# Softmax weights divided before they are turned, values as the stationary operand, and head outputs split in place for the output projection

## The chip, the cores and the metric

The program runs on one core of one Trainium2 chip (trn2). It is one launch. The metric is the device time of that launch in microseconds (us), the median of a few executions. Beside it there is one profiled execution, whose trace is read here.

The engines have short names: PE is TensorE (products; PEld its weight loads), DVE is VectorE, ACT is ScalarE, POOL is GpSimd, SP is SyncE, which issues the DMAs.

## The reference

Two blocks of two layers each run one after the other on 256 tokens of width 1024 in float32. The first block (gated linear attention, a dense and a mixture-of-experts feed-forward) is not touched by the change. Of the second block these parts matter:

```python
def causal_block_attention(score_fn, v):
    def one_block(blk):
        start = blk * BLOCK_Q                      # 128 queries
        s = score_fn(start)
        q_pos = start + jnp.arange(BLOCK_Q)
        s = jnp.where(k_pos[None, :] <= q_pos[:, None], s, -jnp.inf)
        w = jax.nn.softmax(s, axis=-1).astype(v.dtype)
        return jnp.einsum('bhqk,bkhd->bqhd', w, v)

# layer 0, "fox": 16 heads of 64 columns
cum = jnp.cumsum(jax.nn.log_sigmoid(f_logit), axis=1).transpose(0, 2, 1)
s = q_t . k_s * FOX_HEAD_DIM ** -0.5 + cum[t] - cum[s]
mix = o.reshape(B, S, D_MODEL) @ w_o               # 1024 x 1024

# layer 1, "mla": 16 heads, 128 + 64 score columns, 128 value columns
s = (q_nope . k_nope + q_rope . k_rope) * (QK_NOPE_DIM + QK_ROPE_DIM) ** -0.5
mix = o.reshape(B, S, MLA_HEADS * V_HEAD_DIM) @ w_o   # 2048 x 1024
```

Each of the two attentions is followed by its output product with `w_o`, a residual and a layer norm, and then a feed-forward layer whose weights (2816 wide) are streamed from memory.

## The kernel before

**Order of the work.** `stages()` lists the steps of the program. Each engine runs through the same list in its own block of code, in order, and the engines meet at semaphores only. No scheduler moves anything. `Tally` counts how often each semaphore will have been raised when a step begins (`n.g`, `n.act` and so on). The steps around the change are, for layer 0, `fox`, `trs8 "src"`, `out1`, `ln`, and for layer 1, `mla`, `trs16 "src"`, `out2`, `ln`.

**Products of linear layers.** Float32 operands are split into a high half (rounded to fp32r, a TensorE input format) and a low half (the rest). A product is then three fp32r products: high by high, high by low, low by high. Activations stand as `u_hi`/`u_lo` (1024 wide) or `y_hi`/`y_lo` (2048 wide). ACT writes the high half, DVE subtracts it for the low half. Weights come by DMA into `wide` and are split piece by piece, 128 x 1024 each, into the two-deep ring `l_hi`/`l_lo` (the last chunk also into `out_hi`/`out_lo`). Plain float32 products are used in the attentions. In the trace one plain float32 product stands as two MATMUL records, an fp32r product as one.

**Attention.** `HEAD_GROUPS` makes 12 rounds: in rounds 0 to 3 the first 128 queries with four heads each (scores 128 x 128), in rounds 4 to 11 the second 128 queries with two heads each (scores 128 x 256), so that every round has 128 x 512 scores. In round i:

- PE computes the scores of round i into a bank of `G` (two banks), turns the weights of round i-2 (four 128 x 128 transposes into `TB`), and multiplies the turned weights of round i-3 with the values into the banks `A`. The turned weights are the stationary operand, the values the moving one. For fox the scores have a second product that adds the running sum of the gates, with `ncT` as moving operand and a column of the identity, repeated, as the stationary one.
- DVE adds the causal mask while it reads `G` into `probs` (L2457, for mla L2459 with the scale), and takes the row maximum (L2462). `probs` has four buffers.
- ACT copies the turned weights of round i-2 out of `TB` (L1838), then takes the exponential of round i with its row sums (L1863).
- When a bank of `A` is full (`bank_filled`: after rounds 1, 3, 7, 11 for fox; after 0, 1, 2, 3, 5, 7, 9, 11 for mla), `weighted` on DVE takes the reciprocal of the sums (L2474) and multiplies the bank by it into `src` or `src2` (L2475).

**After the attention.** `trs8`/`trs16` turns the finished token rows back (16 or 32 transposes, L898, four at a time into `TB`). For each four, ACT writes the high half (L2132) and DVE the low half (L2811). PE executes filler products between them (`keep_clock`, operand `con`). The output product of `out1` has two chunks of four pieces, each piece 12 products of 512 columns (`out_product`). The one of `out2` has four chunks of four pieces, each 24 products of 256 columns. In the last chunk the first 128 tokens come first, and the layer norm begins on them.

```python
for i in range(GROUPS + 3):          # PE, attention()
    ...                              # scores of round i
    if 2 <= i < GROUPS + 2:
        pe.wait_ge(act_ready, act0 + j + 1)        # exponentials of round j = i - 2
        transposes(tg0 + j, [probs[:, j % PROBS, tok(b)] for b in range(4)])
    if i >= 3:
        last = mm(o, pbT[:, j % 2, k * (t + 1) + b, :], v[:, b, h * vcols:(h + 1) * vcols], b == 0, b == t)
```

## Time and profile before

| | |
|---|---|
| median of 3 runs | 2648.91 us |
| lowest and highest of them | 2639.38 and 2651.41 us |
| the profiled execution | 2649.84 us |
| its span (first to last instruction) | 2648.1 us |
| PE, DVE, ACT busy | 95%, 64%, 49% of the span |
| mean granted TensorE clock | 0.975 |

The profiled execution's time is 1.74 us longer than its span, and 0.93 us above the median. Busy shares are means over the whole program; the attentions and what follows them are a small part of it. The granted clock is 1.0 at 2.4 GHz and 0.5 at 1.2 GHz.

### The profile page before, as it was taken

Reading aid. Unit: us, or ns where it says so; the run is one execution under the profiler, and the core shown is the slowest. Engines: PE = TensorE matmul, PEld = TensorE weight load, DVE = VectorE, ACT = ScalarE, POOL = GpSimd, SP = SyncE. Lnnn points to the kernel's source line nnn. Section 1 sums busy time; section 2 is a strip of 40 time slices with the busy share of each in tenths; the row PEclk is TensorE's granted clock in tenths of the full one; section 3 lists DMA queues with packets and bytes.
Section 4 is the critical chain, followed back from the end, with each engine's and each line's share of the span. In section 5 each row is a group of like instructions: output and inputs, shape, how many; then the busy total and the mean of one; then the engine's idle time right before and its main releaser. Section 6 shows DMA issues by size and latency. Waiting matters only on the chain.

```text
span 2648.1 us, 31868 instructions
## 1 busy us (share of the span) xinstructions
PE 2516.0 (95%) x11824; PEld 1992.5 (75%) x11824; DVE 1700.9 (64%) x1927; ACT 1305.7 (49%) x1659; POOL 108.8 (4%) x119
## 2 busy tenths in 40 slices
PE   6998998999999999999998999989998999999996
PEld 2666884657888888888877888868875887897884
DVE  2456455569999999999986454564455453446455
ACT  1333442327877877878863442444433443444441
POOL 1020001020000000000001000000000000000001
PEclk7999998999999999999999998999999999999998
DMA  8755538838999999999984553245535553336551
GB/s 321 279 212 193 190 135 306 306 133 301 390 367 352 361 342 368 361 334 376 364 313 162 190 180 106 96 167 185 184 121 173 198 173 127 117 102 213 190 182 40
DMA packets 316738, 609.72 MB, mean 230 GB/s; under 512 B 15073, under 2 KB 154369, under 8 KB 309954
## 3 DMA queue, kind: packets, MB, share of 16 engines
q1 hardware_dynamic: 309312, 583.14, 61.9%
q0 software_dynamic: 7024, 23.83, 2.6%
q8 instruction: 79, 1.29, 0.2%
q10 hardware_dynamic: 274, 1.05, 0.1%
q14 instruction: 49, 0.40, 0.0%
HBM read 606.88 MB, written 1.08 MB: 230 GB/s over the span
## 4 chain that ended last, share of the span: by engine, by line
PE 84%; DVE 7%; DMA 4%; ACT 2%; issue 1%; POOL 1%; SPq 0%; DVEq 0%; ACTq 0%
PE G L876 49%; PE A L876 28%; PE TB L876 4%; DMA down<-in_ada_w 1%; PE TB L898 1%; DVE w_lo L2531 1%; POOL small L2333 1%; DMA wide<-in_ffn_w_in 1%; PE TB L1179 1%; DVE small L2860 1%; DVE u_lo L2811 1%; PE TB L1262 1%; DMA down<-in_moe_w_down 1%; DVE x_tok L2849 1%; DVE x_tok L2872 1%
## 5 line engine op out<-in xcount | busy, mean ns | idle before, releaser
L876 PE MATMUL G<-w_hi,u_hi 128*128 128x512 f32 x1584 | 630.0, 398 | 11.8 <-DVE u_lo L2811 6.5
L876 PE MATMUL G<-w_hi,u_lo 128*128 128x512 f32 x1584 | 620.1, 391 | 0.0
L876 PE MATMUL G<-w_lo,u_hi 128*128 128x512 f32 x1584 | 620.0, 391 | 0.0
L2572 DVE TENSOR_TENSOR w_lo<-wide,w_hi 128x1024 fp32r<-128x1024 f32 x352 | 415.4, 1221 | 13.6 <-ACT w_hi L1931 3.5
L1931 ACT ACTIVATE w_hi<-wide 128x1024 fp32r<-128x1024 f32 x352 | 371.3, 1062 | 88.9 <-PE G L876 44.9
L876 PEld LDWEIGHTS G<-w_hi,u_hi 128*128 128x128 f32 x1584 | 299.2, 189 | 76.7 <-DVE w_lo L2531 12.1
L876 PEld LDWEIGHTS G<-w_hi,u_lo 128*128 128x128 f32 x1584 | 299.1, 189 | 64.7
L876 PEld LDWEIGHTS G<-w_lo,u_hi 128*128 128x128 f32 x1584 | 299.3, 189 | 60.1 <-issue 0.2
L876 PE MATMUL A<-w_hi,hidden_hi 128*128 128x512 f32 x792 | 309.6, 391 | 0.0
L876 PE MATMUL A<-w_hi,hidden_lo 128*128 128x512 f32 x792 | 308.5, 390 | 0.0
L876 PE MATMUL A<-w_lo,hidden_hi 128*128 128x512 f32 x792 | 308.2, 389 | 0.0
L2531 DVE TENSOR_TENSOR w_lo<-wide,w_hi 128x1024 fp32r<-128x1024 f32 x220 | 259.6, 1221 | 37.1 <-ACT w_hi L1921 36.5
L1921 ACT ACTIVATE w_hi<-wide 128x1024 fp32r<-128x1024 f32 x220 | 225.1, 1053 | 29.1 <-PE G L876 12.4
L2572 DVE TENSOR_TENSOR w_lo<-down,w_hi 128x1024 fp32r<-128x1024 f32 x176 | 212.7, 1224 | 30.6 <-ACT w_hi L1931 23.8
L2483 DVE TENSOR_TENSOR l_lo<-wide,l_hi 128x1024 fp32r<-128x1024 f32 x96 | 117.5, 1224 | 165.0 <-ACT l_hi L1883 164.9
L1931 ACT ACTIVATE w_hi<-down 128x1024 fp32r<-128x1024 f32 x176 | 184.9, 1063 | 41.6 <-PE G L876 30.7
L2746 DVE TENSOR_TENSOR hidden_lo<-TB,hidden_hi 128x512 fp32r<-128x512 f32 x50 | 34.6, 692 | 262.2 <-ACT hidden_hi L2056 262.2
L1883 ACT ACTIVATE l_hi<-wide 128x1024 fp32r<-128x1024 f32 x96 | 100.5, 1056 | 197.2 <-PE G L876 113.6
L876 PEld LDWEIGHTS A<-w_hi,hidden_lo 128*128 128x128 f32 x792 | 148.7, 188 | 31.2
L876 PEld LDWEIGHTS A<-w_lo,hidden_hi 128*128 128x128 f32 x792 | 148.8, 188 | 30.2
L876 PEld LDWEIGHTS A<-w_hi,hidden_hi 128*128 128x128 f32 x792 | 148.7, 188 | 30.2
L2056 ACT ACTIVATE hidden_hi<-TB 128x512 fp32r<-128x512 f32 x50 | 30.0, 599 | 253.6 <-PE TB L1179 253.6
(347 smaller groups left out, 3272.5 us busy)
## 6 DMA issues: line engine op xcount, KB each, us to landing
down<-in_moe_w_down SPq DMA_DIRECT2D x176, 512.0 KB, 8.0
wide<-in_ffn_w_in SPq DMA_DIRECT2D x88, 1024.0 KB, 7.5
wide<-in_moe_w_gate SPq DMA_DIRECT2D x160, 512.0 KB, 8.3
wide<-in_moe_w_up SPq DMA_DIRECT2D x160, 512.0 KB, 9.1
down<-in_ffn_w_out SPq DMA_DIRECT2D x44, 1024.0 KB, 8.5
down<-in_ada_w SPq DMA_DIRECT2D x40, 1024.0 KB, 7.0
wide<-in_w_in SPq DMA_DIRECT2D x24, 1024.0 KB, 6.9
wide<-in_fox_w_in SPq DMA_DIRECT2D x12, 1024.0 KB, 5.0
```

The lines of the kernel that those rows point to most:

```text
L876: return nc.tensor.matmul(o, lhsT, rhs, start=start, stop=stop, skip_group_check=True)
L898: last = nc.tensor.transpose(TB[:, tg % 2, b * P:(b + 1) * P], block_in, ident)
L1179: last = nc.tensor.transpose(TB[:, (n.tg + j) % 2, f * S + t * P:f * S + (t + 1) * P], hid[:, 0, t, tok(f)], ident)
L1262: last = nc.tensor.transpose(TB[:, unit % 2, tok(f)], gated[:, unit % 2, tok(f)], ident)
L1883: nc.scalar.activation(ring[p % depth], wide[w % RW][:, q * 1024:(q + 1) * 1024], ACT.Copy) \
L1921: nc.scalar.activation(to[:, :], raw, ACT.Copy).then_inc(hi_ready, 1)
L1931: nc.scalar.activation(w_hi[at % RING][:, :], raw, ACT.Copy).then_inc(hi_ready, 1)
L2056: nc.scalar.activation(hth[:, :], TB[:, (n.tg + j) % 2, :], ACT.Copy).then_inc(act_ready, 1)
L2483: V.tensor_tensor(l_lo[at][:, :], wide[(n.w + slots[c]) % RW][:, q * 1024:(q + 1) * 1024], l_hi[at][:, :].bitcast(F32), ALU.subtract).then ...
L2531: V.tensor_tensor(w_lo[to][:, :], raw, w_hi[to][:, :].bitcast(F32), ALU.subtract).then_inc(lo_ready, 1)
L2572: V.tensor_tensor(w_lo[at % RING][:, :], raw_piece(n, at)[0], w_hi[at % RING][:, :].bitcast(F32), ALU.subtract).then_inc(lo_ready, 1)
L2746: V.tensor_tensor(htl[:, :], TB[:, (n.tg + j) % 2, :], hth[:, :].bitcast(F32), ALU.subtract) \
```

## The change

Four things change, for both attentions where nothing else is said.

1. **Weights are divided before they are turned.** `weighted` goes. A new `weights(j)` on DVE takes the reciprocal of the sums of round j and multiplies the 128 x 512 weights in `probs` by it. It stands behind the mask and the maximum of round j+1. The transposes now wait for it (`probs_ready`) and no longer for the exponentials.
2. **Values are stationary.** The product of weights and values has the values as stationary operand and the turned weights as moving one, 128 columns. Its result is turned already: rows are head columns. For fox two neighbouring heads of 64 columns go to the partitions 0 to 63 and 64 to 127 of one bank, and their products alternate.
3. **Head outputs become operands at once.** `trs8 "src"` and `trs16` behind the attentions go, with their transposes and filler. In the round four behind, ACT writes the high half of a full bank (`u_hi` or `y_hi`) behind the exponentials, and DVE the low half behind `weights`. The first two pieces of `w_o` are split within the attention (on ACT behind rounds 8 and 10, on DVE behind rounds 12 and 14), and the first piece of the output product stands on PE ahead of the last product of weights and values. The other pieces of chunk 0 wait for the banks that they read and write.
4. **The gate's sums of fox by one fp32r product.** The sums are written twice by the product with `tri`, to rows 0 to 15 and 32 to 47. ACT rounds them into `nc_parts`; DVE puts the rest into the rows from 32 on. `part_of` has a one in both rows of a head. The second score product of a head is then one fp32r product.

`krz` moves to another buffer, and the table `CLOCK_FILL` is renumbered for the steps that are gone; the fills of the other steps stay, those within the two steps that are gone go with them.

```diff
-        plan += [("kvturn", 0), ("tr8", "x"), ("mla", 0), ("trs16", "src"), ("out2", ("mla", 0))] if i else \
-                [("trs8", "x"), ("fox", 0), ("trs8", "src"), ("out1", ("fox", 0))]
+        plan += [("kvturn", 0), ("tr8", "x"), ("mla", 0), ("out2", ("mla", 0))] if i else \
+                [("trs8", "x"), ("fox", 0), ("out1", ("fox", 0))]
...
+        def heads_halves(fox, t, b):
+
+            at = (slice(None), slice(4 * b, 4 * b + 4), slice(t * P, (t + 1) * P))
+            hi, lo = (v[:, :].rearrange("p (k s) -> p k s", s=S)[at] for v in ((uh, ul) if fox else (yh, yl)))
+            return hi, lo, A[:, 2 * t + b if fox else b, :].rearrange("p (k s) -> p k s", k=4)
...
                     if 2 <= i < GROUPS + 2:
                         j = i - 2
-                        pe.wait_ge(act_ready, act0 + j + 1)
+                        pe.wait_ge(probs_ready, norm0 + j + 1)
                         transposes(tg0 + j, [probs[:, j % PROBS, tok(b)] for b in range(4)])
                     if i >= 3:
                         j = i - 3
                         t, heads = HEAD_GROUPS[j]
+                        if j == GROUPS - 1:
+                            first_piece()
...
-                                o = A[:, 2 * t + h // 8, (h % 8) * FOX_D:(h % 8 + 1) * FOX_D]
+                                o = A[FOX_D * (h % 2):FOX_D * (h % 2) + FOX_D, 2 * t + h // 8, tok(h % 8 // 2)]
                                 v = fv
-                            for b in range(t + 1):
-                                last = mm(o, pbT[:, j % 2, k * (t + 1) + b, :], v[:, b, h * vcols:(h + 1) * vcols],
-                                          b == 0, b == t)
+                            last = mm(o, v[:, b, h * vcols:(h + 1) * vcols], pbT[:, j % 2, k * (t + 1) + b, :],
+                                      b == 0, b == t)
...
                 def piece(c, q, tiles):
+                    if banks and c == 0:
+                        pe.wait_ge(acc_free, n.free - banks + max(banks // 2 + (banks == 4), (kpp * (q + 1) - 1) // 4 + 1))
...
-                        return mm(o, ident[:, h:h + 1].to_broadcast([P, P]), ncT[:, 0:P * (t + 1)], False, True)
+                        return mm(o, part_of[:, h:h + 1].to_broadcast([P, P]), nc_parts[:, 0:P * (t + 1)], False, True)
...
             # ACT, attention(), round i
                         last.then_inc(act_ready, 1)
+                    for at, (j, t, b) in enumerate(banks):
+                        if j == i - 4:
+                            hi, _, bank = heads_halves(fox, t, b)
+                            act.wait_ge(acc_done, n.acc + at + 1)
+                            nc.scalar.activation(hi, bank, ACT.Copy).then_inc(heads_hi, 1)
+                    if i in (GROUPS - 4, GROUPS - 2):
+                        linear(m, (int(i == GROUPS - 2),))
...
             # DVE, attention(), round i
+                    if 1 <= i <= GROUPS:
+                        weights(i - 1, act0)
+                    if i in (GROUPS, GROUPS + 2):
+                        q = (i - GROUPS) // 2
+                        dve.wait_ge(t_done, tg0 + GROUPS - 2 + 2 * q)
+                        linear_rest(m, 0, q)
                     for at, (j, t, b) in enumerate(banks):
                         if j == i - 4:
-                            weighted(n, at, t, b, fox)
+                            hi, lo, bank = heads_halves(fox, t, b)
+                            dve.wait_ge(heads_hi, (0 if fox else 4) + at + 1)
+                            V.tensor_tensor(lo, bank, hi.bitcast(F32), ALU.subtract).then_inc(acc_free, 1)
...
+            def weights(j, act0):
+
+                t, heads = HEAD_GROUPS[j]
+                size = len(heads)
+                sums = slice(heads[0], heads[0] + size)
+                part = probs[:, j % PROBS].rearrange("p (h s) -> p h s", h=size)
+                dve.wait_ge(act_ready, act0 + j + 1)
+                link(V.reciprocal(rinv[:, t, sums], rsum[:, t, sums]))
+                V.tensor_tensor(part, part, rinv[:, t, sums].unsqueeze(2).to_broadcast([P, size, P * (t + 1)]), ALU.mult) \
+                    .then_inc(probs_ready, 1)
```

The next rows show the order on PE around the end of the fox attention, before the change: the end of the last scores and the last rounds (transposes `TB<-con,probs`, values `A<-arena,hidden_T`), what follows it, and the first products of the output product.

```order
L876 MATMUL G<-arena,con 128x256
L898 MATMUL TB<-con,probs 128x128 x4
L876 MATMUL A<-arena,hidden_T 128x64 x4
L898 MATMUL TB<-con,probs 128x128 x4
L876 MATMUL A<-arena,hidden_T 128x64 x4
L898 MATMUL TB<-con,probs 128x128 x4
L876 MATMUL A<-arena,hidden_T 128x64 x8
L898 MATMUL TB<-con,arena 128x128 x16
L876 MATMUL G<-con 128x512
L876 MATMUL A<-l_hi,u_hi 128x512
```

The same place after the change, up to the first products of the first piece of `w_o`:

```order
L885 MATMUL G<-fox_gate_sum_parts,fox_gate_sum_rows 128x256
L907 MATMUL TB<-con,probs 128x128 x4
L885 MATMUL A<-hidden_T,arena 64x128 x4
L907 MATMUL TB<-con,probs 128x128 x4
L885 MATMUL A<-hidden_T,arena 64x128 x4
L907 MATMUL TB<-con,probs 128x128 x4
L885 MATMUL A<-hidden_T,arena 64x128 x4
L885 MATMUL A<-l_hi,u_hi 128x512
```

The 16 transposes of `arena` and the filler on `con` are gone. The 12 products of the first piece stand where the last four products of weights and values stood; those four follow behind them.

On DVE in the fox attention, before the change, two rounds of 256-column scores and a full bank read as follows (mask, maximum, mask, maximum, reciprocal, bank times reciprocal).

```order
L2457 TENSOR_TENSOR probs<-G,con 128x512
L2462 TENSOR_REDUCE small<-probs 128x2
L2457 TENSOR_TENSOR probs<-G,con 128x512
L2462 TENSOR_REDUCE small<-probs 128x2
L2474 RECIPROCAL small<-small 128x8
L2475 TENSOR_TENSOR arena<-A,small 128x512
```

After the change:

```order
L2494 TENSOR_TENSOR probs<-G,con 128x512
L2499 TENSOR_REDUCE small<-probs 128x2
L2521 RECIPROCAL small<-small 128x2
L2522 TENSOR_TENSOR probs<-probs,small 128x512
L2494 TENSOR_TENSOR probs<-G,con 128x512
L2499 TENSOR_REDUCE small<-probs 128x2
L2521 RECIPROCAL small<-small 128x2
L2522 TENSOR_TENSOR probs<-probs,small 128x512
L2511 TENSOR_TENSOR u_lo<-A,u_hi 128x4x128
```

Each round has gained a reciprocal and a multiplication of the weights, and a round with a full bank has the low half of the heads in place of the bank's multiplication.

On ACT in the mla attention after the change (before it, a round had only the first two of these forms: `hidden_T<-TB` and `probs,small`):

```order
L1867 ACTIVATE hidden_T<-TB 128x512
L1894 ACTIVATE probs,small<-probs,small 128x256 x2
L1901 ACTIVATE y_hi<-A 128x4x128
L1867 ACTIVATE hidden_T<-TB 128x512
L1894 ACTIVATE probs,small<-probs,small 128x256 x2
L1921 ACTIVATE l_hi<-wide 128x1024
```

The high half of a bank stands behind the exponentials of its round, and the first split pieces of `w_o` have moved in from behind the loop.

## Rows read from the trace of the kernel before

**Rows 1.** The page: the span, the busy times, the chain by engine.

```profile
span 2648.1 us, 31868 instructions
...
PE 2516.0 (95%) x11824; PEld 1992.5 (75%) x11824; DVE 1700.9 (64%) x1927; ACT 1305.7 (49%) x1659; POOL 108.8 (4%) x119
...
PE 84%; DVE 7%; DMA 4%; ACT 2%; issue 1%; POOL 1%; SPq 0%; DVEq 0%; ACTq 0%
```

**Rows 2.** The chain in order of time, fox and after: start, us, what.

```profile
1689.31 5.59 PE G L876 x48
...
1695.34 1.79 PE G L876 x16
...
1716.76 1.78 PE G L876 x8
1718.54 0.44 PE TB L898 x4
1718.98 0.84 PE A L876 x8
...
1724.88 1.84 PE A L876 x16
...
1734.08 6.20 PE A L876 x24
...
1743.06 8.03 DMA wide<-in_ffn_w_in
...
1754.62 1.14 DVE x_tok L2855
...
1790.41 5.45 PE A L876 x24
```

**Rows 3.** The chain in order of time, mla and its output product.

```profile
2293.24 5.62 PE G L876 x48
...
2322.94 0.89 PE A L876 x8
...
2328.85 1.89 PE A L876 x16
...
2343.32 29.08 PE A L876 x240
```

**Rows 4.** Timeline of DVE in the fox attention, and one split of weights.

```profile
1703.28 0.69 DVE L2457 TENSOR_TENSOR probs<-G,con 128x512 f32<-128x512 f32 x1 [1.65 <-PE G L876]
1704.01 0.69 DVE L2462 TENSOR_REDUCE small<-probs 128x2 f32<-128x512 f32 x1
1704.61 0.19 DVE L2474 RECIPROCAL small<-small 128x8 f32<-128x8 f32 x1
1704.84 0.69 DVE L2475 TENSOR_TENSOR arena<-A,small 128x512 f32<-128x512 f32 x1
...
1741.40 1.23 DVE L3141 TENSOR_TENSOR l_lo<-wide,l_hi 128x1024 fp32r<-128x1024 f32 x1 [1.44 <-ACT l_hi L2146]
```

**Rows 5.** Timeline of ACT in the fox attention, and a split behind it.

```profile
1703.72 0.60 ACT L1838 ACTIVATE hidden_T<-TB 128x512 f32<-128x512 f32 x1 [0.95 <-PE TB L898]
1704.73 0.51 ACT L1863 ACTIVATE probs<-probs,small 128x256 f32<-128x256 f32 x1 [0.41 <-DVE small L2462]
...
1705.63 0.19 ACT L1863 ACTIVATION_READ_ACCUMULATOR probs<-probs,small 128x1 f32 x1
...
1725.42 1.99 ACT L1883 ACTIVATE l_hi<-wide 128x1024 fp32r<-128x1024 f32 x2
```

**Rows 6.** Timeline of PE: two fp32r products of 256 columns.

```profile
1650.35 0.28 PE L876 MATMUL G<-u_hi,l_lo 128*128 128x256 f32 x1
...
1650.47 0.28 PE L876 MATMUL G<-u_hi,l_hi 128*128 128x256 f32 x1
```

**Rows 7.** Windows behind the fox attention: bounds, length, busy (instructions), clock, DMA.

```profile
1727.00:1734.00 7.00, 5.17 (x19) 3.48 (x20) 4.90 (x8) 2.80 (x5) 0.00 (x0) 0.61 0.00 0
1734.00:1740.00 6.00, 6.00 (x25) 4.77 (x24) 2.09 (x2) 1.06 (x1) 0.00 (x0) 0.89 0.01 3
```

More of the change, by code:

```diff
@@ L196 @@
         "kvturn": dict(tg=2),
-        "fox": dict(g=12 + GROUPS, tg=GROUPS, w=6, act=1 + GROUPS, dve=2, acc=4, free=4, src=2, lo=24, lin=18),
-        "mla": dict(g=24 + 24 + GROUPS, tg=2 + 4 + GROUPS, w=7, act=2 + GROUPS, dve=3, pool=2, acc=8, free=8, src=2),
+        "fox": dict(g=12 + GROUPS, tg=GROUPS, w=6, act=1 + GROUPS, dve=2, acc=4, free=4, lo=24, lin=18),
+        "mla": dict(g=24 + 24 + GROUPS, tg=2 + 4 + GROUPS, w=7, act=2 + GROUPS, dve=3, pool=2, acc=8, free=8),
         "ple": dict(g=4, tg=1, w=3, act=2, acc=2, lo=8, lin=6),
@@ L414, in build @@
         fkz = area(BIG + 6144, FOX_H, S)
-        krz = area(3072, 2, S)
-        ncT = area(BIG + 14336, S)
-        fls = area(BIG + 14624, T, FOX_H)
+        krz = pack[:, 2048:2560].rearrange("p (a s) -> p a s", a=2)
+        nc_parts = split_tensor("fox_gate_sum_parts", S, arena_at + 4 * (BIG + 14336))
+        fls = area(BIG + 10240, T, P)
+        part_of = split_tensor("fox_gate_sum_rows", FOX_H, arena_at + 4 * (BIG + 10496))
+        LOW_ROWS = 32
         flt = area(BIG + 14656, T, FOX_H)
@@ L1003, in piece @@
                     return last
+                if first:
+                    pe.wait_ge(lo_ready, n.lo + 1)
+                    piece(0, 0, range(T)).then_inc(lin_used, 1)
+                    return
                 for c in range(chunks - 1):
                     for q in range(4):
+                        if banks and (c, q) == (0, 0):
+                            continue
                         pe.wait_ge(lo_ready, n.lo + 4 * c + q + 1)
@@ L1851, in sum_squares, with attention @@
                     ins.then_inc(act_ready, 1)
-            def attention(tg0, max0):
-                for i in range(GROUPS + 2):
-                    if i >= 2:
+            def attention(n, m, tg0, max0, fox):
+                banks = bank_filled(FOX_D if fox else VH)
+                for i in range(GROUPS + 5):
+                    if 2 <= i < GROUPS + 2:
                         evac(tg0 + i - 2, pbT[:, i % 2])
@@ L2270, in _ @@
                         evac(n.tg + 2 + j, qrT[:, 2 * j:2 * j + 2, :])
-                    attention(n.tg + 6, GROUPS)
+                    attention(n, steps[index + 1][2], n.tg + 6, GROUPS, False)
                 elif kind == "ple":
@@ L2440, in rope, with attention @@
                 return V.tensor_tensor(dst[1], dst[1], t1, ALU.add)
-            def attention(n, g0, tg0, max0, fox):
+            def attention(n, m, g0, tg0, max0, act0, fox):
                 banks = bank_filled(FOX_D if fox else VH)
                 mask = con[:, CONST_COLS["open"][0]:CONST_COLS["causal"][1]]
-                for i in range(GROUPS + 4):
+                for i in range(GROUPS + 5):
                     if i < GROUPS:
@@ L3201, in gate_terms @@
                             dve.wait_ge(act_ready, n.act + 1)
+                            dve.wait_ge(gate_cleared, 1)
                             for t in range(T):
-                                V.scalar_tensor_tensor(out=fls[:, t, :], in0=A[:, t, 0:FOX_H], scalar=0.0, in1=flt[:, t, :],
-                                                       op0=ALU.min, op1=ALU.subtract).then_inc(dve_ready, 1)
-                    V.memset(ncT, 0.0).then_inc(gate_cleared, 1)
+                                for row in (0, LOW_ROWS):
+                                    last = V.scalar_tensor_tensor(out=fls[:, t, row:row + FOX_H], in0=A[:, t, 0:FOX_H],
+                                                                  scalar=0.0, in1=flt[:, t, :],
+                                                                  op0=ALU.min, op1=ALU.subtract)
+                                last.then_inc(dve_ready, 1)
+                        if (c, q) == (4, 3):
+                            low = slice(LOW_ROWS, LOW_ROWS + FOX_H)
+                            dve.wait_ge(gate_turned, 1)
+                            V.scalar_tensor_tensor(out=nc_parts[low, :], in0=A[low, 2, 0:S], scalar=-1.0,
+                                                   in1=nc_parts[low, :].bitcast(F32), op0=ALU.mult, op1=ALU.subtract) \
+                                .then_inc(gate_low, 1)
+                    V.memset(fls, 0.0).then_inc(gate_cleared, 1)
+                    V.tensor_tensor(part_of[:, :], ident[:, 0:FOX_H], ident[:, LOW_ROWS:LOW_ROWS + FOX_H], ALU.add)
                     dve.wait_ge(gate_hi_ready, 1)
```

89 lines of the change are left out of this document (43 added, 46 removed).

## The prediction

> **What bounds the kernel now.** I read the page first. PE is busy for 95% of the span, and 84% of the chain that ended last is PE's [rows 1]. The reader is to see that time is gained only where PE gets less to do, or where PE waits. So I looked next at the chain in order of time at the two attentions and behind them, then at the timelines of DVE and ACT there, and at the clock.
>
> In the fox attention a round with 256-column scores takes 3.06 us, and all of it is PE's: transposes 0.44, values 0.84, scores 1.78 [rows 2]. DVE does a mask and a maximum in that time, 1.4 us, and waits 1.65 us for PE [rows 4]. From the first scores (1689.31) to the end of the last values (1724.88 + 1.84) are 37.4 us. The output product begins only at 1734.08, 7.4 us later, and its first 24 records take 6.20 us, where 24 such records elsewhere take 5.45 [rows 2]. The granted clock says why: 0.61 and 0.89 in the two windows there [rows 7]. So the product starts, for all that follows, 44.8 + 0.75 = 45.5 us after the first scores.
>
> In mla the values end at 2330.74, 37.5 us after the first scores (2293.24), and the output product begins at 2343.32, 50.1 us after them [rows 3].
>
> **The change: the tails.** The transposes, the splits of their results and the filler behind both loops go. This is 7.4 us (plus 0.75 of slow clock) and 12.6 us of path. What takes their place is the chain from the last weights to the output product, which starts inside the loop. To price it I walk the engines through the rounds: each instruction starts when its engine is free and what it waits for has ended, plus 0.04 us for the signal. Done for the kernel before, the walk ends the fox values at 37.2 us (trace: 37.4) and puts the twelfth mask at 32.4.
>
> **The rounds of fox.** PE: the gate's product was plain float32, 8 records in 1.78 us, so 0.445 for each product of two records. An fp32r product of 256 columns takes 0.12 from one start to the next [rows 6]. New scores: 2 x (0.445 + 0.12) = 1.13. With 128 columns (16 records in 1.79, 0.224 a product) no row shows fp32r; it lies between 0.06 and 0.12, I take one record, 0.11, so 4 x 0.335 = 1.35. Values: eight records take 0.84 with 64 moving columns and 0.89 with 128 [rows 2, 3]. Moving columns hardly count there. I take 0.89, the row with as many moving columns as now. PE's round is 1.13 + 0.44 + 0.89 = 2.46.
>
> DVE: mask to maximum 0.73, maximum to reciprocal 0.60, reciprocal to product 0.23 [rows 4], and 0.61 for the product of the weights, as long as the old product of a bank (0.69, with 0.08 of overlap). That is 2.17 a round, in place of 1.33. No row has this product from and to `probs`; the nearest from above is a 128 x 1024 operation, 1.23 [rows 4]. I take 0.69, because the size is the same.
>
> A round with a full bank costs more. DVE's low half waits for ACT's high half, which stands behind the exponentials, which wait for the maximum of the same round: maximum ends at 1.42, exponentials 1.46 to 2.55 (the next ACT instruction can start at 2.48), high half to 3.08 [rows 5], low half 3.12, next mask at 3.73. Behind the waiting DVE stand the next mask and the weights, and PE waits for both. So fox rounds take 2.46 by PE, 2.17 when DVE catches up, or 3.73 with a bank (i = 5, 7, 11). The walk puts fox's twelfth mask at 30.0, 2.4 before the old 32.4. The gate's product gives some 6.9 us of PE work, but DVE takes most of it back.
>
> **The tail of fox.** From the twelfth mask (30.0): bank round 3.73, weights of the last round 0.92, so 34.6; transposes and the values of the eleventh round to 36.0. The first piece of `w_o` (12 records of 0.227 = 2.73; its split ended at 35.8) to 38.7, the last values to 39.6, piece 1 to 42.4. Piece 2 waits: ACT writes the last high half, then splits (1.06), DVE follows (1.23), 42.7. With two pieces done by then, the product starts, in effect, at 42.7 - 5.46 = 37.2. Gain of fox: 45.5 - 37.2 = **8.3 us**.
>
> **Mla.** Its scores keep their 1.73 us and PE its round of 3.06. It has eight full banks, in rounds 4 to 7 and every second one after. A bank round takes 3.73 or more, one without a bank 2.17 to 2.4, since PE has caught up meanwhile. The walk gives masks at 11.6, 15.3, 19.0, 22.8, 26.5, 28.7, 32.7 and 35.1 for rounds 4 to 11; before, the twelfth was at 32.3. The loop loses 2.8 us. Tail: last weights ready at 39.8, values of round 10 until 41.2. The first piece waits for the bank of round 9 (high half behind the last copy on ACT, 41.6; low half 42.3), runs 2.9 us (24 of 240 records in 29.08 [rows 3]), the last values end at 46.15, piece 1 at 49.05, piece 2 starts at 49.2 when it is split. In effect the product starts at 49.2 - 5.8 = 43.4. Gain of mla: 50.1 - 43.4 = **6.7 us**.
>
> **Costed at nothing.** The clearing of `fls`, `part_of`, two more small operations on `fls` and the rest of the sums are some 1 us of DVE in the input product of fox, where PE's products cover them and DVE has room (64% busy over the span [rows 1]); without that cover they would cost that 1 us. `krz` moves a write. Of DMAs none is added. Those of the next feed-forward layer are released by the splits of `w_o`, which move with the pieces: the one at 1743.06 takes 8.03 us, and what it brings stands on DVE ahead of the layer norm at 1754.62 [rows 2]. Before it is asked for 9.0 us after the product's start, behind the split of the fourth piece; in the walk that split ends 7.8 us after the start, so the layer norm moves with the product and the gain is passed on.
>
> **Sum.** 8.3 + 6.7 = 15.0. Against the profiled execution's 2649.84 this gives 2634.8; the median of the runs is 0.93 lower, which gives 2633.9. I say 2634.5.
>
> **A rule against the trace.** The rows say that eight records of values cost 0.84 to 0.89 however few the moving columns [rows 2, 3]. The Trainium skill, "TensorEngine Tiling (Array Packing)", Performance Considerations, recommends just this swap with column tiling where the moving side has 64 columns or fewer, and promises up to twice the speed. The trace of before has no pair of heads on two halves of the columns. By the rule the sum would be 16.8, by the rows 15.0.
>
> **The rivals.**
> - *The two halves run at once* (chance 0.12). Fox values fall from 0.89 to 0.45, PE's round to 2.0, and DVE's 2.17 binds. Walked through, piece 2 starts 1.8 us earlier: 2632.7. For it: the products alternate between the halves. Against it: no row shows overlap. This is what the page of the skill named above would make of it.
> - *Changing the width of the stationary operand costs* (0.12). Each of 12 rounds goes to 64 columns and back. At one record of values, 0.11 us [rows 2], a change, this is 2.6 us: 2637. The same page, Key Properties, says that a change of mode drains the engine; no row here prices it.
> - *The clock falls in the new lulls* (0.12). PE idles 1.1 us three times at each tail, and behind the old fox loop the clock fell after a lull [rows 7]. At half clock one or two pieces last twice as long: 2.7 us for each, so up to 5.5 in sum for both attentions: 2640.
> - *Slower* (0.07). The multiplication of the weights takes as long as the 128 x 1024 row or more. There are 24; DVE binds both loops, so each 0.1 us above 0.69 costs up to 2.4 us. At 1.23 the gain falls to 15.0 - 24 x 0.54 = 2.0; from 1.31 on the kernel is slower. With 1.4 it would be 2652. Against it: the old multiplication of the same size took 0.69 [rows 4].
> - *The fp32r gate product doesn't pay* (0.05). It runs as long as the plain one. Fox's round goes back to 3.06, DVE has slack, and the tails alone are left: 2640.
> - *Forecast* (0.52): 2634.5, by itself 2631 to 2638.
>
> **How the numbers follow.** A measurement of this kernel tells about 0.5% from no change, 13.2 us, so the line lies at 2635.7 on the median. My forecast stands 1.8 us inside it. Of its 0.52 I give 0.38 to faster and 0.14 to within; of the halves at once 0.11 to faster; of changes of width and clock 0.02 and 0.03 to faster, the rest within; the gate to within. Together faster 0.54, within 0.39, slower 0.07. The range goes from 2628 (the halves at once and a fall of the clock fewer behind a layer norm) to 2644 (the clock's case with the widths'), since the runs of before alone reach from 2639 to 2651.
>
> **What would show it.** Right: DVE's new product near 0.69; fox rounds of 2.2 to 2.5 and 3.7; mla rounds of 3.7 with a bank; the first scores to piece 2 in 42.7 (fox) and 49.2 us (mla); the clock at 1.0 there. The prediction is wrong where DVE waits for ACT longer than 1 us in a bank round, where the fox values take 0.45, or where the layer norm does not move with the output product but waits for the DMA of the weights.

## The result, and the profile after

| | before | changed |
|---|---|---|
| median of the runs, us | 2649.16 (2639.38 to 2651.41, 4 runs) | 2634.61 (2630.73 to 2635.28, 4 runs) |
| ratio, 95% interval | | 0.9947 [0.9932, 0.9963] |
| profiled execution, us | 2649.84, span 2648.1 | 2630.73, span 2628.6 |

The median falls by 14.55 us; 14.4 were forecast (2648.91 to 2634.5). The profiled executions lie 19.1 us apart, their spans 19.5. The page of the changed kernel, its first lines and the chain by engine and by line, to read beside [rows 1]:

```profile
span 2628.6 us, 31679 instructions
...
PE 2493.1 (95%) x11714; PEld 1965.0 (75%) x11714; DVE 1706.4 (65%) x1953; ACT 1303.7 (50%) x1659; POOL 110.9 (4%) x119
...
PE 82%; DVE 9%; DMA 4%; ACT 3%; issue 1%; POOL 1%; SPq 0%; DVEq 0%; ACTq 0%
```

PE has lost 110 instructions and 22.9 us of busy time. DVE has gained 26 instructions, and two more of a hundred parts of the chain: in the attentions it now decides.

The chain in order of time through fox and to the layer norm behind it (start, us, what), to read beside [rows 2]:

```profile
1687.00 1.54 PE G L885 x12
...
1702.30 0.49 ACT u_hi L1901
...
1703.42 0.69 DVE probs L2494
...
1718.98 0.49 ACT u_hi L1901
1719.49 0.69 DVE u_lo L2511
...
1720.29 0.70 DVE probs L2522
1721.03 0.65 PE TB L907 x4
1721.69 7.12 PE A L885 x40
1728.83 1.07 ACT l_hi L2184
...
1731.59 9.03 DMA wide<-in_ffn_w_in
...
1741.78 2.36 DVE w_lo L2576 x2
1744.14 1.14 DVE x_tok L2899
```

Three things are to be seen. The chain goes through ACT's high half and DVE in the rounds with a bank, where before it was PE's from end to end. From the last transposes on PE runs without a gap into the output product. And the layer norm stands behind a DMA of weights, as it did before, but this DMA takes 9.03 us where it took 8.03 [rows 2]. The norm's first addition comes 57.1 us after the first scores; before it was 1754.62 - 1689.31 = 65.3 [rows 2]. That is the 8.2 us that fox gives at its norm.

The same chain through mla, to read beside [rows 3]:

```profile
2280.45 3.85 PE G L885 x32
...
2292.24 0.70 DVE probs L2496
...
2293.69 1.09 ACT probs L1894 x4
2294.78 0.49 ACT y_hi L1901
...
2295.90 0.69 DVE probs L2496
...
2299.55 0.69 DVE probs L2496
...
2322.72 4.01 PE A L885 x32
...
2328.40 1.24 DVE l_lo L3185
...
2329.68 15.38 PE A L885 x126
```

The masks stand 3.66 and 3.65 us apart, and the chain of such a round runs mask, maximum, exponentials, high half, low half, mask. The third piece begins at 2329.68, 49.2 us after the first scores.

DVE's timeline in fox, to read beside [rows 4]. The idle time in brackets is the wait that replaced the wait for PE:

```profile
1699.75 0.69 DVE L2494 TENSOR_TENSOR probs<-G,con 128x512 f32<-128x512 f32 x1
1700.48 0.69 DVE L2499 TENSOR_REDUCE small<-probs 128x2 f32<-128x512 f32 x1
1701.08 0.16 DVE L2521 RECIPROCAL small<-small 128x2 f32<-128x2 f32 x1
1701.27 0.69 DVE L2522 TENSOR_TENSOR probs<-probs,small 128x512 f32<-128x512 f32 x1
1702.81 0.69 DVE L2511 TENSOR_TENSOR u_lo<-A,u_hi 128x512 fp32r<-128x512 f32 x1 [0.85 <-ACT u_hi L1901]
1703.42 0.68 DVE L2494 TENSOR_TENSOR probs<-G,con 128x512 f32<-128x512 f32 x1
```

PE's timeline of one fox round:

```profile
1695.44 0.66 PE L885 MATMUL A<-hidden_T,arena 128*64 128x128 f32 x8
1696.03 0.70 PE L885 MATMUL G<-arena 128*128 128x256 f32 x2
1696.38 0.47 PE L885 MATMUL G<-fox_gate_sum_parts,fox_gate_sum_rows 128*128 128x256 f32 x1
1696.68 0.59 PE L885 MATMUL G<-arena 128*128 128x256 f32 x2
1696.93 0.47 PE L885 MATMUL G<-fox_gate_sum_parts,fox_gate_sum_rows 128*128 128x256 f32 x1
1697.23 0.60 PE L907 MATMUL TB<-con,probs 128*128 128x128 f32 x4
```

From start to start: values 0.59, scores 1.20, transposes 0.53; the next round's scores begin 2.32 us after these. Behind the loop the clock is full, where [rows 7] had 0.61 and 0.89 (windows: bounds, length, busy, clock, DMA):

```profile
1721.00:1731.00 10.00, 9.97 (x54) 7.42 (x55) 5.24 (x5) 4.32 (x6) 0.00 (x0) 1.00 0.00 0
1731.00:1745.00 14.00, 14.00 (x63) 11.61 (x62) 8.00 (x8) 6.82 (x7) 0.00 (x0) 1.00 0.96 312
```

**What else the two traces differ by.** The spans differ by 19.5 us: 2.3 arose before fox's first scores (1689.31 and 1687.00), 8.2 from there to fox's norm, 6.7 in mla, and 2.3 more between fox's norm and mla's first scores, on a stretch that the change leaves as it is but for the place of `krz`. Of these last, 1.6 us are a fall of the clock, some 320 us behind fox's first scores, that the trace of before has and that of the changed kernel has not. The same 32 products, in the chain of before, of the changed kernel and of run 10 below, with the clock of a window of 5 us in the first two:

```profile
2011.97 10.51 PE A L876 x32
2000.78 8.89 PE A L885 x32
1995.78 10.49 PE A L885 x32
...
2012.00:2017.00 5.00, 5.00 (x13) 3.38 (x14) 4.03 (x4) 3.70 (x4) 0.00 (x0) 0.67 0.57 193
2001.00:2006.00 5.00, 5.00 (x19) 3.50 (x19) 4.22 (x4) 3.99 (x6) 0.00 (x0) 1.00 0.52 188
```

So the whole way from fox's first scores to the end is 17.2 us shorter in these traces, and 14.9 of them are the two attentions. There is one trace of the kernel before; whether the clock falls at this place in every execution of it is not known.

### The profile page after: what moved, and what is told of

Same layout as the page of the kernel before. It is cut to its first block, busy times and chain, and to the rows that moved or that the text cites. A ratio compares the mean times of both kernels' runs of the same rounds, so it can differ in the third digit from the quotient of the medians.

```text
span 2628.6 us, 31679 instructions
## 1 busy us (share of the span) xinstructions
PE 2493.1 (95%) x11714; PEld 1965.0 (75%) x11714; DVE 1706.4 (65%) x1953; ACT 1303.7 (50%) x1659; POOL 110.9 (4%) x119
## 4 chain that ended last, share of the span: by engine, by line
PE 82%; DVE 9%; DMA 4%; ACT 3%; issue 1%; POOL 1%; SPq 0%; DVEq 0%; ACTq 0%
PE G L885 48%; PE A L885 27%; PE TB L885 4%; DMA down<-in_ada_w 1%; DMA wide<-in_ffn_w_in 1%; PE TB L907 1%; POOL small L2370 1%; DVE w_lo L2576 1%; PE TB L1210 1%; DVE small L2904 1%; DVE u_lo L2855 1%; PE TB L1293 1%; DMA down<-in_moe_w_down 1%; DVE x_tok L2893 1%; DVE x_tok L2916 1%
## 5 line engine op out<-in xcount | busy, mean ns | idle before, releaser
L1959 ACT ACTIVATE w_hi<-wide 128x1024 fp32r<-128x1024 f32 x220 | 225.2, 1053 | 32.3 <-PE G L885 12.7
```

Source lines behind the costliest of these rows:

```text
L1959: nc.scalar.activation(to[:, :], raw, ACT.Copy).then_inc(hi_ready, 1)
```

## The experiments

All are compared with the kernel before, whose median was 2649.16 beside the first run of the changed kernel and 2648.17 to 2648.58 us in the three later sets of runs. "Mask", "piece 2" and "norm" are the times from the first scores to the start of the twelfth mask, of the third piece of the output product, and of the first addition of the layer norm behind the attention, each from the run's own trace.

| run | median, us | ratio, 95% interval | fox mask / piece 2 / norm | mla mask / piece 2 / norm |
|---|---|---|---|---|
| before | 2649.16 | | 32.3 / - / 65.2 | 32.4 / - / 93.4 |
| changed | 2634.61 | 0.9947 [0.9932, 0.9963] | 29.3 / 41.8 / 57.1 | 35.0 / 49.2 / 86.7 |
| changed, again | 2631.69 | 0.9937 [0.9925, 0.9949] | 29.3 / 41.8 / 57.0 | 35.0 / 49.2 / 86.7 |
| 1 gate in plain float32 | 2636.53 | 0.9953 [0.9939, 0.9966] | 32.6 / 44.9 / 59.1 | 35.0 / 49.2 / 86.9 |
| 2 heads in turn | 2631.42 | 0.9939 [0.9925, 0.9953] | 29.3 / 43.2 / 58.4 | 35.0 / 49.2 / 86.6 |
| 3 mla as before | 2642.07 | 0.9977 [0.9966, 0.9987] | 29.3 / 41.8 / 57.0 | 32.4 / - / 94.7 |
| 4 no division | 2626.47 | 0.9915 [0.9901, 0.9929] | 26.2 / 38.0 / 53.3 | 32.9 / 46.6 / 84.1 |
| 5 high half ahead | 2627.27 | 0.9921 [0.9907, 0.9935] | 27.5 / 39.4 / 54.7 | 33.2 / 45.7 / 83.1 |
| 6 first piece behind | 2632.73 | 0.9943 [0.993, 0.9957] | 29.3 / 41.5 / 56.8 | 35.0 / 48.2 / 85.7 |
| 7 low half later | 2626.49 | 0.9925 [0.9912, 0.9937] | 27.7 / 39.6 / 54.9 | 33.2 / 47.3 / 84.6 |
| 8 = 5 and 6 | 2627.11 | 0.9927 [0.9913, 0.9942] | 27.5 / 39.1 / 54.4 | 33.2 / 45.1 / 82.6 |
| 9 one half of columns | 2634.52 (one run) | | 31.1 / 44.3 / 59.3 | 35.0 / 49.3 / 86.6 |
| 10 norm ahead of weights | 2629.66 | 0.9931 [0.9918, 0.9944] | 29.3 / 41.8 / 53.0 | 35.0 / 49.2 / 84.1 |
| 11 = 5 and 10 | 2623.16 | 0.9904 [0.9891, 0.9917] | 27.5 / 39.3 / 50.5 | 33.2 / 45.7 / 80.5 |

The columns of the traces repeat within 0.1 us where nothing there was edited; medians of the same kernel lay 2.9 us apart. So the traces carry the verdicts on the attentions, and the medians the total. All ten runs of the changed kernel have their median at 2633.0, used below. The marks end at the norm, and a median also holds what the clock does behind it: the 32 products shown above took 10.51 us before, 10.33 in run 1 and 10.49 in run 10, and 8.89 or 8.90 in the other eleven traces.

**The changed kernel again.**

> The changed kernel itself once more, so that the versions sent with it are compared with it on the same chip. Theory: 2634.6 as before, within 1.5 us; its trace again with the twelfth mask at 29.3 (fox) and 35.0 (mla) from the first scores. Rival (the prediction came out by a lucky chip): 2637 or more.

The marks came out the same; the median is 2.9 us lower, where 1.5 were allowed. Its profiled execution took 2634.92 us, 4.2 more than the first, and its first scores of fox began at 1691.12, not 1687.00. So some 4 us arise before fox and vary between executions of one kernel, and the 2.3 us of this kind between the traces of before and after tell nothing of the change.

**1. The gate's product in plain float32.**

```diff
-return mm(o, part_of[:, h:h + 1].to_broadcast([P, P]), nc_parts[:, 0:P * (t + 1)], False, True)
+return mm(o, part_of[:, h:h + 1].bitcast(F32).to_broadcast([P, P]), nc_parts[:, 0:P * (t + 1)].bitcast(F32),
+          False, True)
```

> The gate's sums by a plain float32 product of the same operands (fourth part undone); all else as changed. Walk of the rounds: scores of two heads take 1.8 in place of 1.2 us, PE's round in fox grows from 2.3 to 2.95 us, and PE holds the rounds that DVE held: fox 3.2 us longer, mla the same, so about 2637.8 where the changed kernel has 2634.6. Rival (DVE binds the fox rounds anyway): less than 1 us longer.

Scores of a round take 1.83 us again, where they took 1.20. The mask comes 3.2 us later, piece 2 3.1, the norm 2.0: there the DMA ahead of it took 7.92 us and not 9.03. The gate's product is worth 3 us of path at the mask, less than half of the PE time that it removes (0.63 us in each 256-column round, some 6.8 in all) and 2 at the norm. The median lies 3.5 us above that of the ten runs; 1.4 us of that are, by the traces, the fall of the clock behind fox (10.33 against 8.89).

**2. The heads of a pair in turn.**

```diff
-[(k, b) for pair in pairs for b in range(t + 1) for k in (pair, pair + 1)]
+[(k, b) for k in range(len(heads)) for b in range(t + 1)]
```

> The products of values and weights of fox head by head, not alternating between the two halves of the output partitions. Theory (two halves run partly at once, 8 records in 0.59 us): in the 256-column rounds two products of the same half now follow each other, 8 records take 0.75 to 0.95 us, PE's round grows from 2.3 to 2.5 to 2.65 us, fox 1 to 2 us longer, 2635.5 to 2636.6. Rival (a stationary operand of 64 columns is loaded in half the time, whatever the order): 0.59 us as before and no change.

The theory fell. The edit changes the order in the 256-column rounds alone, rounds 4 to 11. The values of round 5:

```profile
1707.88 0.67 PE L885 MATMUL A<-hidden_T,arena 128*64 128x128 f32 x8
1708.47 0.70 PE L885 MATMUL G<-arena 128*128 128x256 f32 x2
```

With four records of one head issued behind four of the other the eight still take 0.59 us, and the mask stays where it was. That the two heads alternate isn't what makes them short. In this trace the clock fell at the end of the loop (windows, columns as above):

```profile
1716.00:1722.00 6.00, 3.76 (x33) 2.61 (x32) 4.90 (x9) 3.75 (x9) 0.00 (x0) 0.84 0.00 0
1722.00:1727.00 5.00, 5.00 (x28) 3.56 (x25) 0.70 (x1) 0.49 (x2) 0.00 (x0) 0.85 0.00 0
```

PE was busy for 3.76 of 6.00 us in the first of them. The last transposes took 1.11 us in place of 0.65, and the norm came 1.3 us later. In the changed kernel's trace the same lulls (PE busy for 3.74 us of 1716.70 to 1722.70) stand at a clock of 1.00. The fall at this place happened in one of thirteen traces with the changed fox; with one trace in this order, whether the order has a part in it is open.

**9. Both heads on one half.** All heads are written to partitions 0 to 63, so that odd heads overwrite even ones and half of the results are lost.

```diff
-o = A[FOX_D * (h % 2):FOX_D * (h % 2) + FOX_D, 2 * t + h // 8, tok(h % 8 // 2)]
+o = A[0:FOX_D, 2 * t + h // 8, tok(h % 8 // 2)]
```

> All heads of fox write their products of weights and values to partitions 0 to 63, so half the heads overwrite the others: leaves out half of the head outputs. One look at the pace of the eight records, now 0.59 us. If products on different halves run at once, they must now take 0.84 us or more; if a stationary operand of 64 columns alone makes them short, 0.59 stays.

PE's timeline of the same round:

```profile
1696.01 1.09 PE L885 MATMUL A<-hidden_T,arena 128*64 128x128 f32 x8
1697.02 0.70 PE L885 MATMUL G<-arena 128*128 128x256 f32 x2
...
1698.23 0.60 PE L907 MATMUL TB<-con,probs 128*128 128x128 f32 x4
1698.76 1.09 PE L885 MATMUL A<-hidden_T,arena 128*64 128x128 f32 x8
```

The eight records now take 1.01 us from start to start, with the same shapes and the same work, and 0.59 on two halves. How the records start shows why. In a window that ends within 0.05 us of the first start, the changed kernel has two records and run 9 has one:

```profile
1708.58 0.33 PE L885 MATMUL A<-hidden_T,arena 128*64 128x128 f32 x2
...
1716.20 0.32 PE L885 MATMUL A<-hidden_T,arena 128*64 128x128 f32 x1
```

On one half the records start one by one (1716.20, .36, .47, .58 and so on, 0.11 us apart from the second on), on two halves in pairs (two at 1708.58, at .74, at .85, at .95 or .96), again 0.11 us from pair to pair. That run 9 writes two heads to one place isn't the reason: its records start no further apart than those of one half in the changed kernel. Products to the two halves of the columns overlap; that alone is worth 0.42 us a round, 1.7 us at the mask, 2.3 at the norm. Scores (1.21) and transposes (0.53) stay as in the changed kernel, so what these have gained over [rows 2] does not hang on the two halves.

**4. No division.** Neither the reciprocal nor the product of the weights is done; the transposes wait for the exponentials.

```diff
-                        pe.wait_ge(probs_ready, norm0 + j + 1)
+                        pe.wait_ge(act_ready, norm0 + j + 1)
...
-                    if 1 <= i <= GROUPS:
-                        weights(i - 1, act0)
```

> Leaves the division by the sums out altogether (no reciprocals, no multiplication of the weights on DVE; transposes wait for the exponentials). Theory (bank rounds are set by DVE's wait for ACT's high half, which stands behind the exponentials, not by the multiplications): fox 3.6 and mla 2.3 us shorter, 2628.7; bank rounds stay at 3.6 us. Rival (the multiplications bind both loops): 24 times 0.84 us, up to 20 us shorter, 2615.

Fox's norm came 3.7 us earlier, mla's 2.6: 6.3 in sum, theory 5.9. Work of 24 x 0.8 us was removed and a third of it came off the path. DVE's wait for ACT grew in its place, from 0.85 to 1.64 us in a bank's round, and the masks of such rounds of fox still stood 3.67 and 3.79 us apart.

**5. The high half ahead.** ACT makes the high half of a bank as the first thing of its round, not behind the exponentials.

```diff
                 for i in range(GROUPS + 5):
+                    for at, (j, t, b) in enumerate(banks):
+                        if j == i - 4:
+                            (high half, as in the change)
                     if 2 <= i < GROUPS + 2:
                         evac(tg0 + i - 2, pbT[:, i % 2])
```

> ACT writes the high half of a full bank at the head of its round, ahead of the copy of turned weights and of the exponentials. Theory (a bank round is long because DVE waits for the high half behind the exponentials): DVE's wait of 0.85 us in each bank round goes, bank rounds fall from 3.65 to some 2.9 us and to PE's own 3.06 in mla; walk: fox 2.5 and mla 3.6 us shorter, 6.1 in sum, about 2628.5 where the changed kernel has 2634.6. Rival (DVE's five operations of a bank round are what costs; the wait has slack behind it): under 2 us.

DVE's timeline in a bank's round:

```profile
1702.50 0.69 DVE L2522 TENSOR_TENSOR probs<-probs,small 128x512 f32<-128x512 f32 x1
1703.11 0.68 DVE L2511 TENSOR_TENSOR u_lo<-A,u_hi 128x512 fp32r<-128x512 f32 x1
1703.71 0.68 DVE L2494 TENSOR_TENSOR probs<-G,con 128x512 f32<-128x512 f32 x1
```

The wait of 0.85 us is gone. Fox's norm comes 2.4 us earlier, mla's 3.6, in sum 6.0 of the 6.1 expected, and the median lies 5.7 below that of the changed kernel.

**7. The low half a round later.** `if j == i - 4` becomes `if j == i - 5` on DVE alone.

> The changed kernel, but VectorE takes the low half of a bank one round later than before (at the head of the round behind the one in which ScalarE makes the high half), so it stands 0.85 us less behind ScalarE; ScalarE's order is left as it is. It is the other cure for the wait that the run with the high half ahead removed. Theory (it is VectorE's standing in a bank's round that prices the loop, wherever it is taken away): the round with a bank falls from 3.73 by up to 0.85 us, but the last bank's low half comes one round later and gives part of it back at the end: fox's LN some 2.3 us earlier, mla's 2.0, the time near 2630.3. Rival (the gain of the other cure came from ScalarE's high half being early for the product, not from VectorE): no gain, 2634 to 2636.

The other cure has nearly the same effect: 2.2 us at fox's norm, 2.0 at mla's (2.3 and 2.0 expected). The median fell by 6.5, or 5.2 against the changed kernel on the same chip, more than the 4.2 of the traces. So the price was DVE standing in the round, and not the moment at which the high half is written. With the later low half mla gains less: the mask comes at 33.2 in both runs, but piece 2, which waits for the last bank, at 47.3 and with run 5 at 45.7.

**6. The first piece behind the loop**, not ahead of the last values.

```diff
-                        if j == GROUPS - 1:
-                            first_piece()
...
                             last.then_inc(acc_done, 1)
+                first_piece()
```

> The first piece of the output product stands behind the last product of weights and values, not ahead of it. Theory (in mla that piece waits for the bank of round 9 and holds up the last values, whose high and low half then come later): mla 1.0 us shorter, fox 0.1, about 2633.5. Rival (the early piece is what covers the splits, as intended): 2.7 to 2.9 us longer for each attention, 2640.

> Both edits together: high half at the head of ACT's round, first piece behind the last values. Theory: fox 2.6 and mla 4.2 us shorter, 6.7 in sum, about 2628. Rival (the two cover the same wait): no better than the better one alone.

The norm came 0.2 us (fox) and 0.9 us (mla) earlier without the early piece. It fills a lull of PE, but the last values, whose bank the third piece waits for, stand behind it. With run 5's edit as well the traces gain 0.8 us more than run 5 alone (0.3 and 0.5 at the norms), and the medians can't tell the two.

**3. Only fox changed.** For mla the old loop, the bank's multiplication, `trs16` and the old start of `out2` are put back.

```diff
-        plan += [("kvturn", 0), ("tr8", "x"), ("mla", 0), ("out2", ("mla", 0))] if i else \
+        plan += [("kvturn", 0), ("tr8", "x"), ("mla", 0), ("trs16", "src"), ("out2", ("mla", 0))] if i else \
```

> Only the fox attention is changed; mla, its turning back and its output product are as in the kernel before. Theory: mla gave 6.7 us, so 2641.3; the trace shows 93.4 us from the first mla scores to the first addition of the layer norm, where the changed kernel has 86.7, and fox's 57.1 us unchanged. Rival (gains of one attention come from the phase of the clock): no steady difference of this size.

2642.07 is 6.1 below the kernel before, and 7.5 to 9.1 above the changed one, by its first median or that of all ten runs. By the traces fox gives 8.2 and mla 6.7 (8.0 against this run, whose DMA ahead of mla's norm took 9.15 us, where before it took 7.99). Within the spread of the medians the two parts add up.

**10. The norm ahead of the weights.** In the changed kernel DVE's timeline behind fox shows the wait that the prediction named as a risk:

```profile
1741.78 2.36 DVE L2576 TENSOR_TENSOR w_lo<-wide,w_hi 128x1024 fp32r<-128x1024 f32 x2 [4.88 <-ACT w_hi L1959]
1744.06 1.21 DVE L2899 SCALAR_TENSOR_TENSOR x_tok<-x_tok,A 128x1024 f32<-128x1024 f32 x1
```

Here `early_rest(behind, 0)` stands behind the first tile's norm:

```diff
-                if before != "moe" and not split_in_tail(index - 1):
+                if before != "moe" and not split_in_tail(index - 1) and not by_tile:
                     early_rest(behind, 0)
-                    if not by_tile:
-                        early_rest(behind, 1)
+                    early_rest(behind, 1)
...
                 if by_tile:
+                    early_rest(behind, 0)
                     early_rest(behind, 1)
```

> The changed kernel, but behind the two attentions VectorE begins the layer norm of the first tile before it splits the first pair of the feed-forward's weights, and does both pairs behind that tile's norm. In the changed kernel it stood 4.88 us for these weights (their DMA lands late) with the product's first tile done. Theory (the norm waits there for a DMA, by VectorE's order alone): the first addition of the norm comes 3.5 to 4 us earlier, at about 53.2 from the first scores in fox and 82.5 in mla; the same work still lies ahead of the feed-forward's first product, so only the idle time in front is won, 1.3 to 1.9 us in each, and the time is near 2631.5. Rival (the product's second tile, or the weights' high half, ends last for the feed-forward): the norm is earlier, the feed-forward is not, 2634.5.

```profile
1736.73 1.22 DVE L2899 SCALAR_TENSOR_TENSOR x_tok<-x_tok,A 128x1024 f32<-128x1024 f32 x1 [3.12 <-PE A L885]
...
1742.63 4.62 DVE L2576 TENSOR_TENSOR w_lo<-wide,w_hi 128x1024 fp32r<-128x1024 f32 x4
```

The norm came 4.1 us earlier in fox and 2.5 in mla. The feed-forward's first product, from the first scores, came at 64.3 and not 66.1 us in fox, and at 95.4 and not 95.6 in mla: DVE has the same work ahead of it either way, and only its idle time in front is won (DVE begins the work that it no longer interrupts at 52.99 in place of 54.78, and at 84.10 in place of 84.37). For fox that is what was expected; in mla norm (82.5 expected, 84.1 measured) and feed-forward gain less, since DVE now waits for the product's first tile until then. In fox the feed-forward's first nine records had run at half clock behind a lull of PE (0.43 us from one to the next, against 0.23), and here the clock did not fall. That won nothing: PE waits for the second tile's norm behind them either way, 0.46 us in the changed kernel and 2.09 here.

The gain of 1.8 us did not last either. At mla's first scores this trace lies 0.1 us ahead of the changed kernel's, each counted from its first scores of fox (593.33 and 593.45 us): on the way the clock fell at the place shown above (10.49 us against 8.89). From fox's first scores to the end 0.4 us are left. The median is 2.0 below that of the changed kernel on the same chip, 3.4 below that of its ten runs, and medians of one kernel differed by 2.9. So the edit's gain is shown up to the feed-forward, and for the whole time it is not shown by this run.

**11. Both edits.**

> The changed kernel with two of the edits tried: ScalarE takes the high half of a bank ahead of its other work of the round, and VectorE takes the first tile's norm ahead of the weights. Theory (two waits in two places, so the gains add): 6 to 7 us by the first as its own run showed, about 3 by the second: near 2624.5. Rival (the product then ends while the weights' DMA still runs, so that what the first edit gains at the norm is lost again at the feed-forward, since this DMA is asked for behind the product's start): 2626 to 2628, no better than the first edit alone.

2623.16 us, the fastest of the study: 8.5 below the changed kernel on the same chip, with an interval of 0.9891 to 0.9917 to the kernel before that lies apart from its 0.9925 to 0.9949. The feed-forward's first product comes at 61.8 (fox) and 91.8 us (mla), 4.2 and 3.8 earlier than in the changed kernel; run 5 alone has 63.7 and 92.1. The gains add. Here the clock fell at neither of the two places, and from the first scores to the end this trace is 7.2 us shorter than the changed kernel's and 1.8 shorter than run 5's: in this pair the norm's edit kept its gain.

## Why the prediction was right

**The sum.** 15.0 us were forecast, 8.3 for fox and 6.7 for mla. The traces show 8.2 and 6.7 at the layer norms, and the medians 14.55. That the medians come so close is partly luck: the second set of runs gives 16.5, and the traces hold 2.3 us more behind fox, most of it from a fall of the clock that the forecast did not look at. (The forecast of 2634.5 stands 1.2 us inside the line of 2635.7, not 1.8; the 1.8 belong to 2633.9. And 4 x 0.335 is 1.34.) The first median lay only 1.1 us below the line of 2635.7, with an interval up to 0.9963; the second, 2631.69 with an interval up to 0.9949, puts the kernel on the faster side of it.

**The walk.** The twelfth mask was put at 30.0 and 35.1 us and came at 29.3 and 35.0; piece 2 was put at 42.7 and 49.2 and came at 41.8 and 49.2. The bank's round of 3.73 was 3.65, DVE's wait in it 0.85. Runs 5 and 7 removed this wait in two ways and gained what the walk said, so it is shown that this wait lengthened the bank rounds, and run 4 shows that the division's work lies mostly beside it.

**The terms that were off.** "I take 0.89, the row with as many moving columns as now": the eight records of values take 0.59. The row was mla's, whose products fill all columns and start 0.11 us apart. Of fox's, two start at once each 0.11 us (run 9 above). So what the Trainium skill, "TensorEngine Tiling (Array Packing)", says of this swap (Performance Considerations), up to twice the speed (Overview, Theoretical Speedup), was borne out: twice by the pace of the starts, and 1.01 over 0.59, a factor of 1.7, with what stands at both ends of the eight. The rival of the two halves, to which the forecast gave 0.12, had this right with its 0.45: four steps of 0.11. It counted on the alternation, and run 2 shows that the order of the heads doesn't matter.

The rival of the changed width came true at the same time, and costs more than it allowed. Beside mla, which never changes width, fox's round has four longer steps from one start to the next: last transpose to first record of the values 0.20 us against 0.11; first to second record on a half 0.16 against 0.11; last record of the values to the first of the scores 0.20 against 0.11; first to second record of these scores 0.32 against 0.22. That is 0.34 a round, 0.15 of it within the 0.59, where 0.22 were allowed. The same page, Key Properties, says that a change of mode drains the engine; the steps stand just at the two changes of width, in runs 1 and 9 too, so neither the fp32r product nor the second half is their reason. That the width is, is argued from the place: no run took the change of width away, and the kernel before, whose stationary width never changes, also had 0.27 for 0.22 in the last of them.

Together: transposes 0.44, values 0.44, scores 1.10 and the four steps' 0.34 make the 2.32 of PE's round, where the forecast had 2.46. Two rivals to which it gave 0.12 each both held, and their errors, -0.45 and +0.34, nearly met: that PE's round came so near the forecast is luck.

**Where 0.9 us of fox went.** The output product of fox began, in effect, at 1728.78 - 5.46 = 1723.3, 36.3 us after the first scores: 9.2 earlier than the 45.5 of before, 0.9 better than forecast. The layer norm got 8.2. The step that failed is "the layer norm moves with the product and the gain is passed on": the DMA took 9.03 us where before it took 8.03. In mla it took 7.89 (before 7.99), and there all was passed on.

**The gate's product** was said to give 6.9 us of PE work of which DVE takes most back. Run 1: some 6.8 us of PE work, of which 3.2 are left at the mask and 2.0 at the norm.

**The clock** stood at 1.00 through both tails of the changed kernel, as the forecast had it, and fell in run 2's tail of fox, as its rival had it, at 1.3 us, where 5.5 were allowed for both attentions. What the forecast did not look at are the places further on: the fall 320 us behind fox's first scores, which the traces of the changed kernel lack, is worth 1.6 us. **The multiplication of the weights** took 0.69 us, which ends the slower rival.

## What to carry to other kernels

When work moves from behind a loop into it, walk the engines through the rounds: what decided here was neither engine's sum of work but one instruction (the low half, 0.85 us of waiting) that held up all that stood behind it on an in-order engine, and moving its partner to the head of the round gave 6 us. Ask behind the loop too what the next stage waits for by order alone: taking the norm ahead of weights that arrive late gave 1.8 and 0.3 us at the next product, no more than the idle time ahead of it. Then follow such a gain to the end of the trace: in run 10 a fall of the clock 320 us behind fox's first scores took nearly all of it back, and the median alone could not have said so. And price a product on half of the columns as part of a pair: with its neighbour's half beside it, it can be far cheaper than the nearest full row says. Price the changes of width apart.

## What the hardware showed beyond the forecast

- Eight float32 records with 64 stationary and 128 moving columns: 1.01 us on one half of the columns, 0.59 over both halves, in either order of issue. Starts on one half are 0.11 us apart in both; the rest stands at the two ends. The same number of records with 128 stationary columns took 0.89.
- The way from 128 stationary columns to 64 and back stands beside 0.34 us more in each round than rounds without it have.
- Of the DMAs of `ffn_w_in` that end ahead of the norms, alike in size (1024 KB), that behind fox took 8.03 us before and 8.86 to 9.07 in ten traces with the changed fox, but 7.92 in run 1, with the gate's product in plain float32. That it was asked for 3.1 us later there doesn't explain it: in run 9, where it was asked for only 0.7 us sooner than in run 1, it took 8.86. That behind mla took 7.82 to 8.09, before too, but 9.15 in run 3. Why is open: no run varied the transfer alone.
- The clock fell in the last lulls of fox in one profiled run of thirteen with the changed fox; and some 320 us behind fox's first scores before and in runs 1 and 10 and in none of the eleven others, with the same work there. What decides it is not shown.
